# A third Strassen block in ten gate and up pairs, and silu as one function of ScalarE

## What is computed

```python
def swiglu(h, w_gate, w_up, w_down):
    return (jax.nn.silu(h @ w_gate) * (h @ w_up)) @ w_down
...
h = rmsnorm(x, norm_ffn_g[l])
x = x + swiglu(h, w_ffn_gate[l], w_ffn_up[l], w_ffn_down[l])
```

## Time and profile before

| | us |
|---|---|
| median of 3 runs (lowest, highest) | 1747.47 (1747.38, 1748.23) |
| the profiled execution, its own time | 1748.19 |
| its span | 1745.9 |
| TensorE busy | 1734.6 (99%), 7905 matmuls |
| TensorE weight loads busy | 1439.8 (82%) |
| VectorE busy | 1327.0 (76%) |
| ScalarE busy | 986.8 (57%) |

### The profile page before, as it was taken

One profiled execution on the slowest core, in us unless ns is written; L12 is line 12 of the kernel. 1 busy time (PEld: TensorE's weight loads), 2 busy tenths in 40 slices (PEclk: granted clock), 3 DMA queues, 4 the chain that ended last, 5 costly groups with the idle time before them and its releaser, 6 DMA issues.

```text
span 1745.9 us, 20385 instructions
## 1 busy us (share of the span) xinstructions
PE 1734.6 (99%) x7905; PEld 1439.8 (82%) x7905; DVE 1327.0 (76%) x1457; ACT 986.8 (57%) x1228; POOL 28.8 (2%) x54
## 2 busy tenths in 40 slices
PE   9999999999999999999999999999999999999998
PEld 7888888888888888888888888888888888888886
DVE  7577687887575757678765579888888888888887
ACT  6767678554555555555465465555555545555554
POOL 1100000000000000000000000000000000000000
PEclk9999999999999999999999999999999999999999
DMA  9565655666565655556865455566566566566663
GB/s 339 174 203 163 212 184 163 201 211 195 158 215 168 217 169 185 174 166 217 271 186 188 140 174 184 191 196 195 196 197 219 187 211 198 183 193 196 214 194 119
DMA packets 176048, 338.23 MB, mean 194 GB/s; under 512 B 10704, under 2 KB 15312, under 8 KB 175696
## 3 DMA queue, kind: packets, MB, share of 16 engines
q1 hardware_dynamic: 173376, 327.98, 59.4%
q0 software_dynamic: 1296, 5.24, 1.0%
q10 hardware_dynamic: 1280, 3.71, 0.5%
HBM read 334.80 MB, written 2.10 MB: 193 GB/s over the span
## 4 chain that ended last, share of the span: by engine, by line
PE 98%; DVE 1%; ACT 0%; DMA 0%; issue 0%; ACTq 0%; POOLq 0%; POOL 0%; DVEq 0%
PE group L486 29%; PE group L488 28%; PE group L487 28%; PE side L486 3%; PE side L487 3%; PE side L488 3%; PE side L549 2%; PE side L683 0%; PE side L667 0%; DMA x_T_in<-in_x_T 0%; PE side L621 0%; PE side L620 0%; PE side L619 0%; DVE x_res L1603 0%; PE side L665 0%
## 5 line engine op out<-in xcount | busy, mean ns | idle before, releaser
L858 ACT ACTIVATE w_hi<-w_raw 128x1024 fp32r<-128x1024 f32 x612 | 618.9, 1024 | 489.7 <-PE group L488 475.7
L1253 DVE TENSOR_TENSOR w_lo<-w_raw,w_hi 128x1024 fp32r<-128x1024 f32 x612 | 707.9, 1179 | 236.7 <-ACT w_hi L858 231.1
L486 PE MATMUL group<-w_hi,x_hi 128*128 128x512 f32 x1460 | 573.3, 393 | 0.6 <-DVE w_lo L1321 0.6
L488 PE MATMUL group<-w_hi,x_lo 128*128 128x512 f32 x1460 | 568.8, 390 | 0.0
L487 PE MATMUL group<-w_lo,x_hi 128*128 128x512 f32 x1460 | 568.2, 389 | 0.0
L486 PEld LDWEIGHTS group<-w_hi,x_hi 128*128 128x128 f32 x1460 | 274.2, 188 | 58.6 <-DVE w_lo L1253 2.3
L488 PEld LDWEIGHTS group<-w_hi,x_lo 128*128 128x128 f32 x1460 | 274.0, 188 | 57.7
L487 PEld LDWEIGHTS group<-w_lo,x_hi 128*128 128x128 f32 x1460 | 274.3, 188 | 55.5
L858 ACT ACTIVATE w_hi<-w_sums 128x1024 fp32r<-128x1024 f32 x98 | 103.9, 1061 | 179.3 <-PE group L488 150.3
L1253 DVE TENSOR_TENSOR w_lo<-w_sums,w_hi 128x1024 fp32r<-128x1024 f32 x98 | 119.9, 1224 | 92.1 <-ACT w_hi L858 92.1
L486 PE MATMUL group<-w_hi,inner_hi 128*128 128x512 f32 x274 | 107.0, 391 | 0.2 <-DVE x_res L1603 0.2
(11 more groups left out here) (329 smaller groups left out, 1792.8 us busy)
## 6 DMA issues: line engine op xcount, KB each, us to landing
w_raw<-in_w_in SPq DMA_DIRECT2D x223, 512.0 KB, 4.2
w_raw<-in_w_ffn_gate SPq DMA_DIRECT2D x88, 512.0 KB, 3.9
w_raw<-in_w_ffn_up SPq DMA_DIRECT2D x88, 512.0 KB, 4.5
w_raw<-in_w_ffn_down SPq DMA_DIRECT2D x88, 512.0 KB, 5.0
w_raw<-in_w_rnn_proj SPq DMA_DIRECT2D x32, 512.0 KB, 4.9
w_raw<-in_w_attn_proj SPq DMA_DIRECT2D x32, 512.0 KB, 4.6
w_raw<-in_w_mix_out SPq DMA_DIRECT2D x32, 512.0 KB, 4.9
w_raw<-in_w_xkv SPq DMA_DIRECT2D x16, 512.0 KB, 3.8
```

The source lines that it names most:

```text
L486: nc.tensor.matmul(out, h, whi[:, s, k, :], start=start, stop=False)
L488: return nc.tensor.matmul(out, l, whi[:, s, k, :], start=False, stop=stop)
L858: nc.scalar.activation(whi[:, s, ks], src[:, ks], ACT.Copy).then_inc(hi_ready[s], 1)
L1253: V_.tensor_tensor(wlo[:, s, ks], src[:, ks], whi[:, s, ks].bitcast(F32), ALU.subtract).then_inc(w_ready[s], 1)
```

## The change

UP_PLAN has three W pairs and five O pairs in place of two and six; it is used by ten of the eleven gate and up pairs, as gate_a 0 has FIRST_UP_PLAN. So these have 22 steps (0 to 21) in place of 20. The sums of activations get a third k pair and buffers of their own. The second half of the fold is made in the last step but one at the latest. ScalarE computes silu itself with the norm's scale in place of tanh, and VectorE's first product and the halved scales fall away; inner_tok also waits for the join of up. The diff, with lines without change cut:

```diff
--- before.py
+++ after.py
@@ -64,7 +64,7 @@
-UP_PLAN = "O0 O1 W3 O2 O4 W5 O6 O7".split()
+UP_PLAN = "O0 O2 W1 O4 W3 O6 W5 O7".split()
@@ -76,7 +76,7 @@
-X_SUMS = [int(_step[1:]) for _step in UP_PLAN if _step[0] == "W"]
+X_SUMS = sorted(int(_step[1:]) for _step in UP_PLAN if _step[0] == "W")
@@ -235,11 +235,14 @@
+        up_both, up_sum = at("up_both", S + 6 * K1, [3, CK, SEQ]), at("up_sums", S, [3, 4, P])
+        us_hi = at("up_sums_hi", S + 10 * K1, [3, 4, P], F32R)
-        STAGE = [region(4 * K1), region(4 * K1)]
+        STAGE = [region(4 * K1), region(6 * K1)]
+        us_lo = at("up_sums_lo", STAGE[1], [3, 4, P], F32R)
-        silu_scale = new("silu_scale", [TT])
@@ -788,7 +790,7 @@
-                    for c, kind, kp in pair_of(first, xhi, xlo, xs_hi, xs_lo, X_SUMS):
+                    for c, kind, kp in pair_of(first, xhi, xlo, us_hi, us_lo, X_SUMS):
@@ -1165,12 +1167,12 @@
-            def gate_tanh(first):
+            def gate_silu(first):
                 wait_taken(act, GI[first])
                 for tt in range(TT):
-                    last = nc.scalar.activation(silu[:, tt, :], fold[:, 0, tt, :], ACT.Tanh, scale=hrstd["x2"][:, tt:tt + 1])
-                last.then_inc(sem("tanh"), 1)
+                    last = nc.scalar.activation(silu[:, tt, :], fold[:, 0, tt, :], ACT.Silu, scale=rstd["x2"][:, tt:tt + 1])
+                last.then_inc(sem("silu"), 1)
@@ -1191,10 +1193,10 @@
-                                sums_hi(xs_hi[:, :, :, :], x_sum[:, :, :, :])
+                                sums_hi(us_hi[:, :, :, :], up_sum[:, :, :, :])
@@ -1302,11 +1304,6 @@
-            def halve(name):
-                dve.wait_ge(sem("rstd_" + name), 1)
-                then(V_.tensor_scalar(hrstd[name][:, :], rstd[name][:, :], 0.5, None, ALU.mult))
-                then(V_.tensor_tensor(silu_scale[:, :], hrstd[name][:, :], rstd[name][:, :], ALU.mult))
@@ -1408,7 +1405,7 @@
                     then(V_.tensor_tensor(fold[:, 0, 1, :], fold[:, 1, 0, :], P7, ALU.subtract))
-                if at_ is not None and c == at_ + 2:
+                if at_ is not None and c == min(at_ + 2, len(STEPS[first]) - 2):
                     V_.tensor_tensor(fold[:, 1, 1, :], Q5, fold[:, 0, 1, :], ALU.subtract)
@@ -1676,17 +1673,13 @@
-            def gate_silu():
+            def inner_tok(second):
                 made[0] += 1
-                dve.wait_ge(sem("tanh"), made[0])
-                marks["silu"] = marked(V_.scalar_tensor_tensor(silu[:, :, :], silu[:, :, :], 1.0, fold[:, 0], ALU.add, ALU.mult))
-
-            def inner_tok():
-
-                dve.wait_ge(sem("vector_chain"), marks["silu"])
+                dve.wait_ge(sem("silu"), made[0])
+                wait_taken(dve, GI[second])
                 for tt in range(TT):
-                    last = V_.scalar_tensor_tensor(stage[0][:, tt, :], fold[:, 1, tt, :], silu_scale[:, tt:tt + 1], silu[:, tt, :], ALU.mult, ALU.mult)
+                    last = V_.scalar_tensor_tensor(stage[0][:, tt, :], fold[:, 1, tt, :], rstd["x2"][:, tt:tt + 1], silu[:, tt, :], ALU.mult, ALU.mult)
@@ -1707,18 +1700,17 @@
                                 variance("x2")
-                                halve("x2")
+                                dve.wait_ge(sem("rstd_x2"), 1)
                             if c == 0:
                                 dve.wait_ge(sem("x2_lo"), KG - 1)
-                                picked = [x[:, :, :].rearrange("p (j b) t -> p j b t", b=NB)[:, 1:3, 2:4, :].bitcast(F32) for x in (xhi, xlo)]
-                                then(V_.tensor_tensor(both[:, :, :, :], picked[0], picked[1], ALU.add))
-                                sums_of(x_sum, both)
+                                picked = [x[:, :, :].rearrange("p (j b) t -> p j b t", b=NB)[:, 0:3, 2:4, :].bitcast(F32) for x in (xhi, xlo)]
+                                then(V_.tensor_tensor(up_both[:, :, :, :], picked[0], picked[1], ALU.add))
+                                sums_of(up_sum, up_both)
                             if c == 2:
-                                sums_lo(xs_lo[:, :, :, :], x_sum[:, :, :, :], xs_hi[:, :, :, :])
+                                sums_lo(us_lo[:, :, :, :], up_sum[:, :, :, :], us_hi[:, :, :, :])
                         if j > 0:
                             if c == 0:
-                                gate_silu()
-                                inner_tok()
+                                inner_tok(("up_" + part, j - 1))
```

More of the change, by code:

```diff
@@ L1193, in _ @@
                             if c == 1:
-                                sums_hi(xs_hi[:, :, :, :], x_sum[:, :, :, :])
+                                sums_hi(us_hi[:, :, :, :], up_sum[:, :, :, :])
                         if j > 0:
                             if c == 0:
-                                gate_tanh(("gate_" + part, j - 1))
+                                gate_silu(("gate_" + part, j - 1))
                             if c == 3:
@@ L1206, in _ @@
                         if c == 0 and q == 0:
-                            gate_tanh(("gate_" + part, groups - 1))
+                            gate_silu(("gate_" + part, groups - 1))
                         if c == 3 and q == 0:
@@ L1738, in _ @@
                         if c == 0 and q == 0:
-                            gate_silu()
-                            inner_tok()
+                            inner_tok(("up_" + part, groups - 1))
                         if c == 3 and q == 0:
```

## The result

| | before | changed |
|---|---|---|
| median of 6 runs each (lowest, highest), us | 1747.81 (1747.38, 1748.23) | 1761.47 (1760.81, 1761.91) |
| the profiled execution, us | 1748.19 | 1761.69 |
| its span, us | 1745.9 | 1759.4 |
| TensorE busy, us (matmuls) | 1734.6 (7905) | 1733.7 (7875) |
| VectorE busy, us | 1327.0 | 1354.6 |

The changed kernel is slower by 13.7 us, a ratio of 1.0079 (95% interval 1.0069 to 1.0089). The forecast was 1760.5, in a range from 1754.5 to 1766.

The account below looks back on a forecast made before the run. TensorE was taken to set the pace, with VectorE close behind. The terms -6.8 + 13.2 + 5.0 + 1.6 = +13.0 us gave 1760.5 us from a median of 1747.47, in a range from 1754.5 to 1766.

Parts of the forecast that it names:

- Saved matmuls: In ten gate and up pairs, 21 matmuls for 24 in three times 0.2267 us each: -6.8 us of TensorE.
- Hand-over: End of ten pairs: the first join is ready late, TensorE stands 1.21 us plus 0.11 restart each, +13.2 us.
- Middle of summed pairs: Step 10 of seven pairs: VectorE's rest is 0.61 us late, 0.72 with restart, +5.0 us.
- gate_a 0: Its sums cover three k pairs instead of two, so the longer operations delay W3's steps: +1.6 us (1.0 to 2.0).
- No debt: VectorE's wait for ScalarE at the rest of D (1.01 us) remains, so no pair hands lateness to the next.
- Silu at nothing: ScalarE's Silu takes the same time as tanh, has 1.9 us to spare, and its table load is hidden: no cost.
- a sign of being wrong: The forecast said it would be wrong if ScalarE's Silu is what inner_tok waits for.
- Hence nothing: The down pairs behind (down_a 0, down_b 0) start their second part afresh too, so no cost there.
- Rival (1): VectorE's 5.5 idle us take in the net 3.2 us and no pair waits: -5.2, 1742.3 us; chance 0.06.
- (2): Rival: only the hand-over costs, the middle of summed pairs doesn't: +8.0, 1755.5 us; chance 0.10.
- (3): Rival: only the middle of summed pairs costs, not the hand-over: -0.2, 1747.3 us; chance 0.05.
- Rival (4): VectorE's waits stay as long and the whole 3.2 us lengthens each of ten pairs: about 1781 us; chance 0.05.

Follow-up runs that it names:

- e7: The changed kernel with fold and joins a step earlier, last inner sums in step 11, gate_a 0's variance in steps 7 and 8: 1743.27 us, ratio 0.9976.
- e3: The changed kernel with VectorE's order in step 20 changed: first join before the fold's last operation, second before the next rest; 1754.42 us, ratio 1.0037.
- e5: The changed kernel with ScalarE's copy of P1, VectorE's fold and both joins moved a step earlier at a pair's end; 1748.67 us, ratio 1.0006.
- e4: The changed kernel with VectorE's last operation of the inner sums moved from step 6 to step 11; 1756.85 us, ratio 1.0050.
- e1: The kernel before with the silu part alone: ScalarE's Silu for tanh, VectorE's 128x1024 product gone, plans as before; 1747.72 us, ratio 1.0000.
- e2: The changed kernel with tanh and VectorE's product back, so the third W block alone; 1761.93 us, ratio 1.0081.
- e8: e2 with one more 128x1024 VectorE operation (1.25 us) that changes nothing, at the start of each pair; 1767.04 us, ratio 1.0115.

## Why the prediction was right, by its own steps

- **Saved matmuls, -6.8 us.** 30 matmuls fewer (7905 to 7875). Where nothing stands, gate_b 0 takes 41.48 us (e7) for 42.16 before: 0.68 a pair.
- **Hand-over, +13.2.** 1.21 us and 0.10 to 0.11 for the restart in ten pairs. Each term: fold 2.50 after D (2.55 in the pair shown), 0.72 and 0.72 (0.73 forecast), 0.61, 0.82 (0.83), join 1.22, start 0.05. e3 took half of it away and e5 all of it (12.8 with what came back at down_a 0).
- **Middle of summed pairs, +5.0.** 0.60 and 0.11, seven times; e4 took 4.6 away and left the restart.
- **gate_a 0, +1.6.** Stands of 0.67, 0.28 and 0.34 us and three restarts: 1.60; from its first transposes to gate_a 1's it is 47.45 us for 45.84. The lengths of the longer operations came out as extrapolated (1.753 and 0.558 us).
- **No debt.** The rest of D waits 0.98 us for ScalarE in the new pair; e1, e2 and e8 take, give and overdraw that room, and the time follows it.
- **Silu at nothing.** That holds for the time, but not for the reason given, in one pair. ScalarE and VectorE at its first use, in step 0 of gate_a 1, and VectorE's next rest of D:

```profile
1075.44 1.06 ACT L860 ACTIVATE w_hi<-w_raw 128x1024 fp32r<-128x1024 f32 x1 [1.66 <-PE group L490]
1076.52 1.28 ACT L1174 ACT_TABLE_LOAD   x1
1077.82 1.34 ACT L1174 ACTIVATE stage<-fold,rstd_x 128x512 f32<-128x512 f32 x2
...
1079.19 1.41 DVE L1682 SCALAR_TENSOR_TENSOR stage<-fold,rstd_x,stage 128x512 f32<-128x512 f32 x2 [1.43 <-ACT stage L1174]
...
1088.32 1.23 DVE L1255 TENSOR_TENSOR w_lo<-w_sums,w_hi 128x1024 fp32r<-128x1024 f32 x1 [1.01 <-ACT w_hi L860]
```

There is one table load of 1.28 us for all eleven pairs, and 710 ns for 128x512, tanh's own. In the ten other pairs VectorE doesn't wait for Silu. Here it waits 1.43 us, which the forecast named as a sign of being wrong. Its 1.9 us to spare are those of a pair whose hand-over is late, where ScalarE is done 1.3 us into the pair and VectorE asks at 3.3. gate_a 1 follows gate_a 0, which keeps its plan and its early join: VectorE asks at 2.6 and Silu ends at 4.0. The wait costs no time, because VectorE still waits 1.01 us for ScalarE at the next rest of D, and TensorE has no stand inside this pair; in e1 the same wait of 1.43 us stands there. The drain of 1380 ns that the Trainium skill names beside the load ("ScalarE: Activation LUTs", What ACT_TABLE_LOAD costs) doesn't show: the split before ends at 1076.50, the load begins at 1076.52 and Silu at 1077.82.
- **Small misses.** The ledger gave 13.0; the profiled executions differ by 13.5, from gate_a 0's first transposes to the end by 13.2 (709.4 and 722.7 us), and the medians by 13.7. Of the 1.0 us by which 1760.5 was short, 0.3 is the base, 1747.47 in the three runs shown and 1747.81 in six. The summed pairs are 1.40 us longer in the mean of seven and not 1.36, about 0.3 in all; gate_a 3 has 1.41, with a stand of 1.25 at the hand-over for 1.21. "Hence nothing" for down_a 0 held in the changed kernel (a stand of 0.2 us, as in the kernel before), but the margin was gone: e2, e5 and e7 stand 0.6 to 0.8 longer there.

Rival (1), free time is free time, is refuted by e1 to e5: VectorE has over 4 us free in gate_a 3 of the changed kernel (40.58 of 44.70) and is late twice. Rivals (2) and (3), one of the two places alone, fall to e4 and e3, which each took their own place away. Rival (4), the debt, falls to e8.

## What to carry to other kernels

A second engine with free time absorbs new work only up to the next point at which it must be on time; so list, for each release that the bound engine waits for, what stands ahead of it in the other engine's list, and add the new work there. When a plan is packed tighter, work that used to be spread over its tail (here the two halves of a fold) piles up ahead of the release: look at what is ordered before the release that doesn't have to be. Here a fold that starts 1.1 us sooner, and two smaller moves, turned a loss of 13.7 us into a gain of 4.3, with the same operations.

## What the runs showed that was not expected

- A stand of TensorE costs about 0.1 us beyond itself, whatever its length: the second matmul follows 0.33 to 0.34 us after the first instead of 0.23, behind stands of 0.28 us as behind 1.25, and in e4 even where A's first matmul comes with no stand at all (at down_a 0 it is 0.31). For short stands, as at B and C in gate_a 0, this is a quarter of the price.
- A wait in the profile is shorter than the stand: it counts 10.5 us for ten waits at the hand-over, where the starts of matmuls give 12.1, and it has none for the stands of 0.05 to 0.07 at step 8. Stands are to be read from starts.
